# Cross-attention keys and queries projected with tokens on partitions, and attention root factors by token block

## The chip, the cores and the metric

The kernel runs on one core of one Trainium2 chip. TensorE (PE in the profile) multiplies, VectorE (DVE), ScalarE (ACT) and GpSimd (POOL) work on tiles of 128 partitions in SBUF, SyncE (SP) issues the loads. The metric is the device time of one execution in microseconds; of several runs the median counts.

## The reference, cut to what matters

One sequence of 256 tokens with 2048 features goes through two blocks: a feed-forward layer, a mixer of attention and gated linear attention, a cross-attention to 256 memory tokens, another feed-forward layer, a recurrent layer and a differential attention. The change touches the cross-attention and the norms of queries and keys in the two other attentions.

```python
def rms_norm(x, g):       # the second block's rms_norm_2 has the same form
    y = x * rsqrt(mean(x * x, axis=-1) + 1e-6)
    return y * g

def cross_attention(h, m, w_q, w_k, w_v, q_norm, k_norm, w_o):
    B, S, _ = h.shape
    M = m.shape[1]
    q = rms_norm((h @ w_q).reshape(B, S, N_XATTN_HEADS, HEAD_DIM).transpose(0, 2, 1, 3), q_norm)
    k = rms_norm((m @ w_k).reshape(B, M, N_XATTN_HEADS, HEAD_DIM).transpose(0, 2, 1, 3), k_norm)
    v = (m @ w_v).reshape(B, M, N_XATTN_HEADS, HEAD_DIM).transpose(0, 2, 1, 3)
    s = jnp.einsum("bhqd,bhkd->bhqk", q, k, preferred_element_type=jnp.float32) * (HEAD_DIM ** -0.5)
    p = jax.nn.softmax(s, axis=-1)
    o = jnp.einsum("bhqk,bhkd->bhqd", p, v.astype(jnp.float32)).astype(h.dtype)
    return o.transpose(0, 2, 1, 3).reshape(B, S, XATTN_W) @ w_o
# called with h = rms_norm(x, xattn_norm) and m = rms_norm(mem, mem_norm); 4 heads of 128
```

## The kernel before

All work hangs on weight units. A unit is 128 x 1024 of a weight matrix in fp32, 512 KB. SP loads it into one of four slots (`w_raw`, ring of four), ACT rounds it to its high half (`split`, L1034), DVE subtracts for the low half (L1510), and TensorE multiplies high by high, high by low and low by high. ACT and DVE are three units ahead of TensorE (`LEAD`); each engine's work that is not a split is put between the splits by the slot j of the unit at which its program names it. Semaphores (`handoffs`) pass results on, and every engine runs its own program strictly in order, so a wait on an engine holds all that stands behind it.

A projection has one of two forms. In the feature form (`unit`, `unit2`, L541 to L544) the weights are stationary and the result has features on partitions: for each of eight 128 x 128 tiles one matmul of 512 columns (high and low half of the activations) with the high weights, and one of 256 columns with the low ones. ACT then copies one half of the bank (`part_out`, L1054), DVE adds the other (`take`, L1533) and multiplies with the token's norm factor (L1535), which had to be spread over all partitions by a matmul of ones with a diagonal (`spread`, L631). In the token form (`unit_tokens`, L581 to L583) the activations are stationary and the result has tokens on partitions, one bank of 512 features for each of two token blocks b: twelve matmuls of 512 columns a unit.

In `cross`, memk (the keys' projection, 8 units) and xq (the queries', 8 units) have the feature form, and memv (the values', 8 units) the token form. Since keys and queries lie with features on partitions, the sum of squares over a head's features is a matmul with a column of ones (`sums`, L638, eight issues, sixteen records). For the keys POOL takes the root, DVE makes eight diagonals (L1978), TensorE spreads them (L949, two issues of 512 columns) and DVE multiplies the keys (L1926). For the queries the root stays by token and goes into the softmax: into the largest score (`largest`) and into the exponential's scale (`power`). The scores (L915) stand ahead of memv's unit 3, the turning of the probabilities (`turn`, L927) ahead of units 6 and 7, the mixes (L971) behind memv. Then comes xo, the output projection.

In both other attentions (mixa, four pairs of heads in 48 units, and att, eight iterations of 16 units) queries and keys already have tokens on partitions. The tables AT_A and AT_D set at which slot a step runs: "rope0" and "rope1" square (ACT) and rotate (DVE, L1687 to L1694) one token block each, "sum" reduces the squares of both blocks in one instruction (DVE, L1701) and adds the epsilon (L1703), POOL takes the root of all eight values (L2204), "scale" multiplies the keys by it (ACT, L1131, four instructions), "face" turns queries and keys (PE, eight transposes, L666).

## Time and profile before

| | us |
|---|---|
| median of 3 runs | 3347.47 |
| lowest, highest | 3344.51, 3347.66 |
| the profiled execution | 3342.44 |
| its span in the profile | 3340.7 |
| PE, DVE, ACT, POOL busy | 3288.2, 2234.1, 1719.0, 394.4 |
| mean granted clock of TensorE | 0.998 |

The span runs from the first to the last instruction, and the profiled execution took 1.7 us more than its span. A busy PE does not mean that it is at its peak: a matmul's end is modelled, and consecutive starts tell the step. Where the profile names a releaser, it is the one that came last.

### The profile page before, as it was taken

Reading aid. Unit: us, or ns where it says so; the run is one execution under the profiler, and the core shown is the slowest. Engines: PE = TensorE matmul, PEld = TensorE weight load, DVE = VectorE, ACT = ScalarE, POOL = GpSimd, SP = SyncE. Lnnn points to the kernel's source line nnn. Section 1 sums busy time; section 2 is a strip of 40 time slices with the busy share of each in tenths; the row PEclk is TensorE's granted clock in tenths of the full one; section 3 lists DMA queues with packets and bytes.
Section 4 is the critical chain, followed back from the end, with each engine's and each line's share of the span. In section 5 each row is a group of like instructions: output and inputs, shape, how many; then the busy total and the mean of one; then the engine's idle time right before and its main releaser. Section 6 shows DMA issues by size and latency. Waiting matters only on the chain.

```text
span 3340.7 us, 55144 instructions
## 1 busy us (share of the span) xinstructions
PE 3288.2 (98%) x18134; PEld 2829.4 (85%) x18134; DVE 2234.1 (67%) x3280; ACT 1719.0 (51%) x2554; POOL 394.4 (12%) x422
## 2 busy tenths in 40 slices
PE   8999999999999999999999999999999999999999
PEld 7888888887888878888888888888888888888888
DVE  7666666676655867666665677787556667665566
ACT  5444444455544655444444456774444445555554
POOL 1000000010023301000000001220333341100000
PEclk9999999999999999999999999999999999999999
DMA  6566666564555655566666655556545455555555
GB/s 229 185 201 184 192 189 189 184 188 145 170 158 163 195 152 161 186 189 187 189 190 188 187 178 178 192 176 189 160 155 156 152 157 177 178 168 176 170 169 164
DMA packets 273914, 592.48 MB, mean 177 GB/s; under 512 B 19856, under 2 KB 163472, under 8 KB 273696
## 3 DMA queue, kind: packets, MB, share of 16 engines
q1 hardware_dynamic: 272672, 587.12, 57.0%
q10 hardware_dynamic: 1152, 4.19, 0.3%
q8 instruction: 52, 0.85, 0.1%
q14 instruction: 38, 0.31, 0.0%
HBM read 589.14 MB, written 2.10 MB: 177 GB/s over the span
## 4 chain that ended last, share of the span: by engine, by line
PE 76%; issue 17%; DVE 4%; POOL 1%; ACT 1%; DMA 0%; SPq 0%; POOLq 0%; ACTq 0%
PE bank L542 42%; PE bank L541 10%; PE bank L544 10%; PE bank L581 3%; PE bank L583 3%; PE bank L582 3%; PE bank L769 2%; DVE w_low L1510 2%; PE bank L781 1%; DVE normed L1555 1%; POOL root_qk L2204 1%; ACT w_high L1034 1%; POOL work L2224 0%; DVE residual L1545 0%; PE bank L736 0%
## 5 line engine op out<-in xcount | busy, mean ns | idle before, releaser
L1510 DVE TENSOR_TENSOR w_low<-w_raw,w_high 128x1024 fp32r<-128x1024 f32 (+1 forms) x1120 | 1376.1, 1237 | 642.3 <-ACT w_high L1034 625.2
L1034 ACT ACTIVATE w_high<-w_raw 128x1024 fp32r<-128x1024 f32 (+1 forms) x1120 | 1166.5, 1044 | 777.2 <-PE bank L583 403.5
L542 PE MATMUL bank<-normed,w_high 128*128 128x512 f32 x4032 | 1286.4, 398 | 12.0 <-DVE w_low L1510 9.0
L542 PE MATMUL bank<-mixed,w_high 128*128 128x512 f32 x2496 | 791.6, 396 | 4.3 <-DVE increment L1542 4.3
L542 PEld LDWEIGHTS bank<-normed,w_high 128*128 128x128 f32 x4032 | 620.6, 189 | 13.6 <-issue 9.0
L541 PE MATMUL bank<-normed,w_low 128*128 128x256 f32 x2016 | 562.1, 279 | 0.0
L544 PE MATMUL bank<-normed,w_low 128*128 128x256 f32 x2016 | 560.0, 278 | 0.0
L541 PEld LDWEIGHTS bank<-normed,w_low 128*128 128x128 f32 x2016 | 379.3, 188 | 92.2
L581 PE MATMUL bank<-w_high,normed 128*128 128x512 f32 x1120 | 451.3, 403 | 2.0 <-DVE w_low L1510 1.1
L1054 ACT ACTIVATE parts<-bank 128x256 f32<-128x256 f32 x384 | 147.6, 384 | 592.0 <-PE bank L542 591.9
L544 PEld LDWEIGHTS bank<-normed,w_low 128*128 128x128 f32 x2016 | 380.0, 189 | 85.0
L583 PE MATMUL bank<-w_high,normed 128*128 128x512 f32 x1120 | 437.6, 391 | 0.0
L582 PE MATMUL bank<-w_low,normed 128*128 128x512 f32 x1120 | 437.0, 390 | 0.0
L542 PEld LDWEIGHTS bank<-mixed,w_high 128*128 128x128 f32 x2496 | 382.5, 189 | 6.8 <-issue 4.0
L541 PE MATMUL bank<-mixed,w_low 128*128 128x256 f32 x1248 | 347.4, 278 | 0.0
L544 PE MATMUL bank<-mixed,w_low 128*128 128x256 f32 x1248 | 346.1, 277 | 0.0
L541 PEld LDWEIGHTS bank<-mixed,w_low 128*128 128x128 f32 x1248 | 234.3, 188 | 57.0
L544 PEld LDWEIGHTS bank<-mixed,w_low 128*128 128x128 f32 x1248 | 234.7, 188 | 53.0 <-issue 0.2
L1533 DVE TENSOR_TENSOR increment<-bank,parts 128x256 f32<-128x256 f32 x252 | 106.9, 424 | 223.0 <-ACT parts L1054 223.0
L583 PEld LDWEIGHTS bank<-w_high,normed 128*128 128x128 f32 x1120 | 210.5, 188 | 45.3
L581 PEld LDWEIGHTS bank<-w_high,normed 128*128 128x128 f32 x1120 | 210.9, 188 | 42.9 <-issue 1.7
L582 PEld LDWEIGHTS bank<-w_low,normed 128*128 128x128 f32 x1120 | 211.1, 188 | 40.5
(293 smaller groups left out, 2291.5 us busy)
## 6 DMA issues: line engine op xcount, KB each, us to landing
w_raw<-w_att SPq DMA_DIRECT2D x128, 512.0 KB, 3.6
w_raw<-w_up1a SPq DMA_DIRECT2D x64, 512.0 KB, 4.2
w_raw<-w_up1b SPq DMA_DIRECT2D x64, 512.0 KB, 4.0
w_raw<-w_up2a SPq DMA_DIRECT2D x64, 512.0 KB, 4.0
w_raw<-w_up2b SPq DMA_DIRECT2D x64, 512.0 KB, 4.0
w_raw<-w_rg SPq DMA_DIRECT2D x64, 512.0 KB, 3.8
w_raw<-w_hg SPq DMA_DIRECT2D x64, 512.0 KB, 3.6
w_raw<-w_hg SPq DMA_DIRECT2D x128, 256.0 KB, 2.8
```

Source lines behind the costliest of these rows:

```text
L541: nc.tensor.matmul(banks[b][:, 0:S], lo, x[:, 0:S], start=False, stop=False)
L542: last = nc.tensor.matmul(banks[b][:, :], hi, x, start=starts and k == 0, stop=stop)
L544: last = nc.tensor.matmul(banks[b][:, 0:S], lo, x[:, 0:S], start=False, stop=False)
L581: nc.tensor.matmul(banks[b][:, :], x_hi, hi, start=starts and k == 0, stop=False)
L582: nc.tensor.matmul(banks[b][:, :], x_hi, lo, start=False, stop=False)
L583: last = nc.tensor.matmul(banks[b][:, :], x_lo, hi, start=False, stop=stops and k == UT // 4 - 1)
L769: last = nc.tensor.matmul(b_out[:, c * P:(c + 1) * P], B[:, 2 + hd, b * P:(b + 1) * P], rhs[:, hd, b * P:(b + 1) * P], start=True, stop=True)
L781: last = nc.tensor.matmul(b_out[:, n * S:(n + 1) * S], gw[:, t * P:(t + 1) * P], C[:, k, :], start=k == 0, stop=k == 1)
L1034: A_(wh[slot][:, 0:width], raw[slot][:, 0:width], ACT.Copy).then_inc(wh_done, 1)
L1054: A_(parts[b], banks[b][:, S:2 * S], ACT.Copy).then_inc(part_ready, 1)
L1510: TT(wl[slot][:, 0:width], raw[slot][:, 0:width], wh[slot][:, 0:width].bitcast(F32), ALU.subtract).then_inc(wl_done, 1)
L1533: TT(inc[:, b, :], gemm[b][:, 0:S], part[b], ALU.add).then_inc(evacuated, 1)
```

## The change

memk and xq go over to the token form. memk's banks are `mem_banks` = (p_a, p_b), xq's are `gemm`, and memv takes `mem_banks` again. `load_tokens` loads memk and xq in pieces as it did memv. Keys: ACT squares the two banks, DVE sums the squares by head and adds the epsilon (`row_sums`), which is scaled by the raw variance of the token (`row_eps`), so that the token's norm factor needs no multiplication at all; POOL takes the root of eight; DVE multiplies the banks by it into `key_rows`; TensorE turns them by eight transposes (`turn_rows`) ahead of xq's unit 5; ACT copies them to `KX`. Queries: ACT and DVE copy one bank each, ACT squares both, TensorE turns the unscaled rows ahead of memv's unit 1, ACT copies them with both gains as a scale, and the root stays by token. Both spreads, both column sums by matmul, the keys' diagonals and their spread, `part_out` and `take` of the two phases are gone. The steps from the scores on move forward by one unit of memv.

In both attentions "sum" becomes "sum0" and "sum1", one for each token block, with half the elements each: sum0 runs right behind rope0 and sum1 where sum was. POOL takes two roots of four values, and ACT's scaling waits for each block's own.

On PE in the cross-attention, the second place ahead of which a step of the keys stands (xq's units). Before, behind xq's unit 5 (L542 is the feature form; `diag` and `squares` hold the diagonals):

```order
L541 MATMUL bank<-mixed,w_low 128x256
L542 MATMUL bank<-mixed,w_high 128x512
L949 MATMUL bank<-diag,ones 128x512 [waits mem_diagonal]
L949 MATMUL bank<-squares,ones 128x512
L542 MATMUL bank<-mixed,w_high 128x512 [waits evacuated,wl_done]
L544 MATMUL bank<-mixed,w_low 128x256
```

After, behind xq's unit 4 (L584 to L586 are the token form, `constants` the identity, `work` the rows of keys):

```order
L584 MATMUL bank<-w_high,mixed 128x512
L585 MATMUL bank<-w_low,mixed 128x512
L586 MATMUL bank<-w_high,mixed 128x512
L939 MATMUL bank<-constants,work 128x128 [waits mem_scaled,rms_low]
L939 MATMUL bank<-constants,work 128x128 x7
L584 MATMUL bank<-w_high,mixed 128x512 [waits wl_done]
L585 MATMUL bank<-w_low,mixed 128x512
```

The matmuls of ones with the diagonals are gone, and eight transposes stand one unit earlier.

On PE at the beginning of memv. Before, the column sums stand behind its unit 1:

```order
L582 MATMUL bank<-w_low,normed 128x512
L583 MATMUL bank<-w_high,normed 128x512
L638 MATMUL bank<-ones,squares 128x1 [waits cross_squared,mem_varied]
L638 MATMUL bank<-ones,squares 128x1 x7
L581 MATMUL bank<-w_high,normed 128x512 [waits wl_done]
L582 MATMUL bank<-w_low,normed 128x512
```

After, the queries' transposes stand behind its unit 0, and the scores (L920) behind its unit 1:

```order
L586 MATMUL bank<-w_high,normed 128x512
L939 MATMUL bank<-constants,work 128x128 [waits cross_also_kept,cross_kept,rms_varied]
L939 MATMUL bank<-constants,work 128x128 x7
L584 MATMUL bank<-w_high,normed 128x512 [waits wl_done]
...
L586 MATMUL bank<-w_high,normed 128x512
L920 MATMUL bank<-mem_keys,work 128x256 [waits cross_gained,cross_squared,mem_keyed]
L920 MATMUL bank<-mem_keys,work 128x256 x3
L920 MATMUL bank<-mem_keys,work 128x256 [waits cross_gained]
L920 MATMUL bank<-mem_keys,work 128x256 x3
```

The column sums are gone; the transposes wait for the copies of the banks that xq's last unit has just finished.

On DVE in an iteration of att, slots 8 and 9. Before, from the last of rope0's products on:

```order
L1690 TENSOR_TENSOR diag<-bank,work 128x4x16
L75 REGISTER_ALU
L1694 TENSOR_TENSOR work<-work,diag 128x4x32 [waits dve_order]
...
L1687 TENSOR_TENSOR work<-bank,work 128x512 [waits att_squared]
L1688 TENSOR_TENSOR diag<-bank,work 128x4x16
L1690 TENSOR_TENSOR diag<-bank,work 128x4x16
...
L1694 TENSOR_TENSOR work<-work,diag 128x4x32 [waits dve_order]
...
L1510 TENSOR_TENSOR w_low<-w_raw,w_high 128x1024 [waits wh_done]
L1701 TENSOR_REDUCE sum_qk<-squares 128x8
...
L1703 TENSOR_TENSOR variance_qk<-sum_qk,eps_by_token 128x8 [waits dve_order]
...
L1510 TENSOR_TENSOR w_low<-w_raw,w_high 128x1024 [waits wh_done]
```

After:

```order
L1701 TENSOR_TENSOR diag<-bank,work 128x4x16
...
L1705 TENSOR_TENSOR work<-work,diag 128x4x32 [waits dve_order]
...
L1714 TENSOR_REDUCE sum_qk<-squares 128x4 [waits dve_order]
...
L1717 TENSOR_TENSOR variance_qk<-sum_qk,eps_by_token 128x4 [waits dve_order]
...
L1698 TENSOR_TENSOR work<-bank,work 128x512 [waits att_squared]
L1699 TENSOR_TENSOR diag<-bank,work 128x4x16
L1701 TENSOR_TENSOR diag<-bank,work 128x4x16
...
L1705 TENSOR_TENSOR work<-work,diag 128x4x32 [waits dve_order]
...
L1521 TENSOR_TENSOR w_low<-w_raw,w_high 128x1024 [waits wh_done]
L1714 TENSOR_REDUCE sum_qk<-squares 128x4
...
L1717 TENSOR_TENSOR variance_qk<-sum_qk,eps_by_token 128x4 [waits dve_order]
```

A reduction of four sums and an addition now stand between the two ropes, and behind the split of slot 9 only the second four are summed.

```diff
-        scores, mixes = (p_a, p_b, p_bc, p_o), (p_bc, p_o, p_t, p_sum)
+        scores, mixes = (*gemm, p_bc, p_o), (p_bc, p_o, p_t, p_sum)
+        mem_banks = (p_a, p_b)
...
-                                    *passes("wout"), ("memk", 8, 4), ("xq", 8, 4), ("memv", 8, 0), ("xo", 8, 0),
+                                    *passes("wout"), ("memk", 8, 0), ("xq", 8, 0), ("memv", 8, 0), ("xo", 8, 0),
...
-                16: [(("rope0", 1), 0)], 17: [(("rope1", 1), 0)], 18: [(("weigh", 0), 0)], 19: [(("sum", 1), 0)],
+                16: [(("rope0", 1), 0), (("sum0", 1), 0)], 17: [(("rope1", 1), 0)], 18: [(("weigh", 0), 0)], 19: [(("sum1", 1), 0)],
...
-                8: [("gate", 1), ("rope0", 0), ("rope1", 0)], 9: [("sum", 0)], 10: [("oturn", 1)], 11: [("scale", 0), ("store", 1)],
+                8: [("gate", 1), ("rope0", 0), ("sum0", 0), ("rope1", 0)], 9: [("sum1", 0)], 10: [("oturn", 1)], 11: [("scale", 0), ("store", 1)],
...
-                if name == "memv":
+                if name in ("memk", "xq", "memv"):
+                    row = 8 if name == "memv" else 0
                     for j in range(units):
-                        load_tokens(q0 + j // RING, j % RING, j // RING, 2 * (j % RING))
+                        load_tokens(q0 + j // RING, j % RING, src[row + j // RING:row + 8:2], 2 * (j % RING))
                     continue
...
+                def turn_rows(rows, banks, done):
+                    for hd in range(HEADS_X):
+                        for b in range(NB):
+                            last = nc.tensor.transpose(banks[hd // 2][:, hd % 2 * S + b * P:hd % 2 * S + (b + 1) * P],
+                                                       rows[:, b, hd * P:(hd + 1) * P], C_("ident"))
+                        if hd % 2:
+                            last.then_inc(done, 1)
...
                     normed("memk", j)
-                    if j == 2:
-                        spread(rms, NORMED["memk"], S)
                     if j == 4:
+                        pe.wait_ge(rms["varied"], NORMED["memk"] + 1)
                         sum_squares("xq")
-                    if j == 6:
-                        spread(rms, NORMED["xq"], S)
-                    unit2(q0, j, g0, XN, True)
+                    unit_tokens(q0 + j // RING, j % RING, 2 * j, XN, mem_banks, j == 0, j == 7)
...
-                    if j == 3:
-                        sums(mem, 0, [((t,), b) for t in range(4) for b in range(NB)])
-                    if j == 6:
-                        pe.wait_ge(mem["diagonal"], 1)
-                        for r in range(2):
-                            nc.tensor.matmul((p_bc, p_o)[r][:, :], ones[:, :], mem_diag[r], start=True,
-                                             stop=True).then_inc(mem["spread"], 1)
-                    unit2(q0, j, g0, Y, True)
+                    if j == 0:
+
+                        pe.wait_ge(evacuated, g0)
+                    if j == 5:
+                        pe.wait_ge(mem["scaled"], 2)
+                        turn_rows(key_rows, (p_bc, p_o), mem["turned"])
+                    unit_tokens(q0 + j // RING, j % RING, 2 * j, Y, gemm, j == 0, j == 7)
...
+                    if j == 1:
+                        pe.wait_ge(rms["varied"], NORMED["xq"] + 1)
+                        pe.wait_ge(crs["kept"], 1)
+                        pe.wait_ge(crs["also_kept"], 1)
+                        turn_rows(query_rows, (p_t, p_sum), crs["turned"])
                     if j == 2:
-                        pe.wait_ge(mem["varied"], 1)
-                        sums(crs, 0, [((t,), b) for t in range(4) for b in range(NB)])
-                    if j == 3:
                         for hd in range(HEADS_X):
                             score(hd)
-                    if j >= 6:
-                        turn(2 * j - 12)
-                        turn(2 * j - 11)
-                    unit_tokens(q0 + j // RING, j % RING, 2 * j, XN, gemm, j == 0, j == 7)
+                    if j in (5, 6):
+                        turn(2 * j - 10)
+                        turn(2 * j - 9)
+                    unit_tokens(q0 + j // RING, j % RING, 2 * j, XN, mem_banks, j == 0, j == 7)
...
-                    act.wait_ge(att["rooted"], it + 1)
                     for b in range(NB):
+                        act.wait_ge(att["rooted"], it * 2 + (b + 1))
...
-                    if j == 1:
-                        act.wait_ge(taken, g0 - takes["xq"])
-                        square(mem, 0, A[:, :, :], 4)
-                    if evacuates("xq", j, True):
-                        k = j - 2 if j < RING else j // 2
-                        part_out(q0, j, g0 + k, k % 2)
+                    if j == 0:
+                        act.wait_ge(pe_unit, q0 * RING)
+                        for b in range(NB):
+                            A_(sq[:, 2 * b:2 * b + 2, :], mem_banks[b][:, :], ACT.Square).then_inc(mem["squared"], 1)
+                    if j == 5:
+                        for r in range(2):
+                            act.wait_ge(mem["turned"], r + 1)
+                            A_(KX[:, 2 * r:2 * r + 2, :], (p_bc, p_o)[r][:, :], ACT.Copy).then_inc(mem["keyed"], 1)
                 q0, g0, _, _ = place["memv"]
                 for j in range(8):
                     ahead("memv", q0, j, 8, True)
                     if j == 0:
-                        act.wait_ge(taken, g0 - takes["memv"])
-                        act.wait_ge(mem["summed"], 1)
-                        square(crs, 0, B[:, :, :], 4)
-                        A_(Dm[:, :, :], B[:, :, :], ACT.Copy, scale=V_("xattn_q_norm")).then_inc(crs["gained"], 1)
-                    if j in (4, 5):
-                        power(2 * j - 8)
-                        power(2 * j - 7)
-                    if j >= 6:
-                        copy_probs(2 * j - 12)
-                        copy_probs(2 * j - 11)
+                        act.wait_ge(pe_unit, q0 * RING)
+                        A_(query_rows[:, 0, :], gemm[0][:, :], ACT.Copy).then_inc(crs["kept"], 1)
+                        for b in range(NB):
+                            if b:
+                                act.wait_ge(crs["also_kept"], 1)
+                            A_(sq[:, 2 * b:2 * b + 2, :], gemm[b][:, :], ACT.Square).then_inc(crs["squared"], 1)
+                    if j == 1:
+                        for r in range(2):
+                            act.wait_ge(crs["turned"], r + 1)
+                            A_(Dm[:, 2 * r:2 * r + 2, :], (p_t, p_sum)[r][:, :], ACT.Copy,
+                               scale=cross_gain[:, 0:1]).then_inc(crs["gained"], 1)
+                    if j in (3, 4):
+                        power(2 * j - 6)
+                        power(2 * j - 5)
...
-                if step == "sum":
-                    own.did(nc.vector.reduce_sum(sum_qk[:, :], sq[:, :, :].rearrange("p a (c d) -> p (a c) d", c=2), AX.X))
-                    own.settle()
-                    TT(var_qk[:, :], sum_qk[:, :], eps_qk[:, :], ALU.add).then_inc(att["varied"], 1)
+                if step in ("sum0", "sum1"):
+                    b = int(step[-1])
+                    of = slice(4 * b, 4 * b + 4)
+                    own.did(nc.vector.reduce_sum(sum_qk[:, of], sq[:, 2 * b:2 * b + 2, :].rearrange("p a (c d) -> p (a c) d", c=2),
+                                                 AX.X))
+                    own.settle()
+                    TT(var_qk[:, of], sum_qk[:, of], eps_qk[:, of], ALU.add).then_inc(att["varied"], 1)
...
+                def row_eps(name, dst):
+
+                    dve.wait_ge(rms["rooted"], NORMED[name])
+                    variance(rms, NORMED[name], [(0, NB)], [1.0 / D], [EPS])
+                    dve.wait_ge(rms["varied"], NORMED[name] + 1)
+                    own.did(TS(dst[:, :].rearrange("p (b c) -> p b c", b=NB), var[:, 0:NB].unsqueeze(2).broadcast_to([P, NB, 4]),
+                               P * EPS, None, ALU.mult))
+                    own.settle()
+
+                def row_sums(h, eps):
+
+                    dve.wait_ge(h["squared"], 2)
+                    own.did(nc.vector.reduce_sum(sum_qk[:, :], sq[:, :, :].rearrange("p a (c d) -> p (a c) d", c=2), AX.X))
+                    own.settle()
+                    TT(var_qk[:, :], sum_qk[:, :], eps[:, :], ALU.add).then_inc(h["varied"], 1)
...
+                    if j == 1:
+                        row_sums(mem, eps_qk)
                     if j == 3:
-                        variance(mem, 0, [(0, 8)], [1.0 / P], [EPS])
-                    if j == 5:
                         dve.wait_ge(mem["rooted"], 1)
-                        for c in range(8):
-                            last = TS(mem_diag[c // 4][:, c % 4 * P:(c % 4 + 1) * P], C_("ident"), rstd[:, c:c + 1],
-                                      None, ALU.mult)
-                        last.then_inc(mem["diagonal"], 1)
-                    if j >= 6:
-                        keys(j - 6)
+                        for b in range(NB):
+                            TT(key_rows[:, b, :].rearrange("p (h d) -> p h d", h=HEADS_X),
+                               mem_banks[b].rearrange("p (h d) -> p h d", h=HEADS_X),
+                               root_qk[:, 4 * b:4 * b + 4].unsqueeze(2).broadcast_to([P, HEADS_X, P]),
+                               ALU.mult).then_inc(mem["scaled"], 1)
...
+                    if j == 0:
+                        dve.wait_ge(pe_unit, q0 * RING)
+                        nc.vector.tensor_copy(query_rows[:, 1, :], gemm[1][:, :]).then_inc(crs["also_kept"], 1)
+                    if j == 1:
+                        row_sums(crs, eps_x)
+                    if j in (2, 3):
+                        largest(2 * j - 4)
+                        largest(2 * j - 3)
+                    if j in (4, 5):
+                        weigh(2 * j - 8)
+                        weigh(2 * j - 7)
...
-                pool.wait_ge(att["varied"], it + 1)
-                PT_(root_qk[:, :], var_qk[:, :], mhalf[:, :], ALU.pow).then_inc(att["rooted"], 1)
+                for b in range(NB):
+                    of = slice(4 * b, 4 * b + 4)
+                    pool.wait_ge(att["varied"], it * 2 + (b + 1))
+                    PT_(root_qk[:, of], var_qk[:, of], mhalf[:, of], ALU.pow).then_inc(att["rooted"], 1)
```

## Rows read from the trace of the kernel before

**Rows 1.** Page, part 1; windows view (length, busy by engine, granted clock, DMA).
```profile
PE 3288.2 (98%) x18134; PEld 2829.4 (85%) x18134; DVE 2234.1 (67%) x3280; ACT 1719.0 (51%) x2554; POOL 394.4 (12%) x422
...
1216.00:1220.00 4.00, 3.95 (x9) 2.08 (x10) 1.87 (x2) 0.00 (x0) 0.00 (x0) 0.63 0.37 113
```

**Rows 2.** PE timeline, cross-attention: start us, us, operation, count, [idle before, releaser].
```profile
1174.91 0.39 PE L542 MATMUL bank<-normed,w_high 128*128 128x512 f32 x1
1176.29 0.67 PE L631 MATMUL bank<-diag,ones 128*128 128x256 f32 x2 [0.98 <-DVE diag L1629]
1176.61 0.58 PE L542 MATMUL bank<-normed,w_high 128*128 128x512 f32 x1
...
1202.78 1.84 PE L638 MATMUL bank<-ones,squares 128*128 128x1 f32 x16
...
1212.70 0.39 PE L542 MATMUL bank<-mixed,w_high 128*128 128x512 f32 x1
1216.05 2.08 PE L949 MATMUL bank<-diag,ones 128*128 128x512 f32 x2 [2.96 <-DVE squares L1978]
1217.92 1.54 PE L949 MATMUL bank<-squares,ones 128*128 128x512 f32 x2
...
1224.63 0.40 PE L542 MATMUL bank<-mixed,w_high 128*128 128x512 f32 x1
1225.97 0.50 PE L581 MATMUL bank<-w_high,normed 128*128 128x512 f32 x1 [0.93 <-DVE increment L1533]
```

**Rows 3.** Timeline of DVE, POOL, ACT and PE, one iteration of att.
```profile
2931.22 1.22 DVE L1701 TENSOR_REDUCE sum_qk<-squares 128x8 f32<-128x1024 f32 x1
2932.47 0.17 DVE L1703 TENSOR_TENSOR variance_qk<-sum_qk,eps_by_token 128x8 f32<-128x8 f32 x1
2932.57 1.23 DVE L1510 TENSOR_TENSOR w_low<-w_raw,w_high 128x1024 fp32r<-128x1024 f32 x1
...
2932.72 2.57 POOL L2204 TENSOR_TENSOR root_qk<-variance_qk,minus_half 128x8 f32<-128x8 f32 x1 [10.57 <-DVE variance_qk L1703]
...
2933.04 1.06 ACT L1034 ACTIVATE w_high<-w_raw 128x1024 fp32r<-128x1024 f32 x1 [2.12 <-PE bank L583]
2935.32 1.28 ACT L1131 ACTIVATE work<-work,root_qk 128x128 f32<-128x128 f32 x4 [1.22 <-POOL root_qk L2204]
...
2935.34 0.39 PE L583 MATMUL bank<-w_high,normed 128*128 128x512 f32 x1
2936.65 1.09 PE L666 MATMUL bank<-constants,work 128*128 128x128 f32 x8 [0.93 <-ACT work L1131]
```

**Rows 4.** PE waits of 2760 to 3260 us: us in total, times, longest.
```profile
PE bank L666 <- ACT work L1131: 7.0, 8, 0.9
```

**Rows 5.** PE timeline: the feature form in memk, then the token form in memv.
```profile
1169.57 0.40 PE L542 MATMUL bank<-normed,w_high 128*128 128x512 f32 x1
...
1243.01 0.39 PE L581 MATMUL bank<-w_high,normed 128*128 128x512 f32 x1
1247.55 0.39 PE L583 MATMUL bank<-w_high,normed 128*128 128x512 f32 x1
```

**Rows 6.** Loads of 1150 to 1262 us: count, KB, median us to landing.
```profile
w_raw<-w_mem SPq DMA_DIRECT2D x16, 512.0 KB, 3.6
```

**Rows 7.** Groups by line (busy us, mean ns, idle before); DVE timeline.
```profile
L927 PE MATMUL bank<-constants,work 128*128 128x128 f32 x16 | 2.3, 279 | 2.4 <-DVE work L1948 2.3
...
2939.61 0.69 DVE L1706 COPY work<-bank 128x512 f32<-128x512 f32 x1
```

**Rows 8.** POOL timeline: a root of eight, and a root of four.
```profile
792.02 1.64 POOL L2204 TENSOR_TENSOR root_qk<-variance_qk,minus_half 128x8 f32<-128x8 f32 x1 [31.67 <-DVE variance_qk L1703]
...
2398.63 1.01 POOL L2230 TENSOR_TENSOR root_heads<-variance_heads,minus_half 128x4 f32<-128x4 f32 x1 [13.73 <-DVE variance_heads L1796]
```

**Rows 9.** PE timeline of mixa, second half of its units.
```profile
882.11 1.09 PE L666 MATMUL bank<-constants,work 128*128 128x128 f32 x8 [1.40 <-ACT work L1131]
...
903.83 0.87 PE L682 MATMUL bank<-constants,work 128*128 128x128 f32 x6 [0.22 <-DVE work L1733]
```

99 lines of the change are left out of this document (39 added, 60 removed).

## The prediction, made before the changed kernel ran

> **What bounds the kernel now.** I read the page first: TensorE is busy for 98% of the span [rows 1], so time is saved only where TensorE stands still or does work that can go. Next the waits of PE, which say where it stands still, then PE's timeline round the cross-attention, where two consecutive starts give the true step (a matmul's modelled end overlaps the next start by 0.16 us), and last the other engines' timelines round each wait. In the cross-attention the reader is to see four interruptions between units that are none of the projection's work [rows 2]. In both other attentions it is one and the same wait: PE stands before the transposes of L666 for ACT's scaling, and ACT stands for POOL's root [rows 3, 4].
>
> **Keys and queries in token form: the units themselves.** Sixteen units change form. A feature unit is 8 x (512 + 256) columns, a token unit 12 x 512: the same 6144. Two feature units take 5.34 + 0.23 = 5.57 us, 2.785 each; in the token form 20 steps take 4.54 us, 0.227 each, 2.72 a unit [rows 5]. Just behind foreign work the token step is nearer 0.23, so I take 0.05 instead of 0.065: 16 x 0.05 = 0.8 us gained, bounds 0 and 1.0. The loads of memk and xq get memv's form; the sixteen loads of `w_mem`, eight of each form, have a median of 3.6 us to landing against the lead of a ring of four units [rows 6]: nothing.
>
> **What goes from PE's path.** (a) The first spread: 0.98 us of wait, 0.16 of overlap, 0.32 of matmul, 1.5 in all; the second has no wait, 0.3 [rows 2]. What is late next is unit 3's low half, whose split stands ahead of this wait in DVE's program; the splits behind it come earlier too, since DVE loses its own wait for POOL's root. (b) The column sums L638, twice 1.84 us of busy time, 1.7 each on the path: 3.4. (c) The keys' spread: from 1212.93 (last matmul 1212.70 + 0.23) to 1219.3 (1217.92 + 1.54 less the overlap), 6.4 us, 3.1 of it waiting for DVE's eight diagonals, the rest four matmuls at a granted clock of 0.63 [rows 1, 2]. (d) The wait for the last evacuation ahead of memv, 1225.97 - 1224.86 = 1.1 [rows 2]. Sum (a) to (d) with the units: 1.8 + 3.4 + 6.4 + 1.1 + 0.8 = 13.5 us.
>
> **What comes onto it.** Sixteen transposes. Eight L666 transposes are busy for 1.09 us [rows 3], sixteen L927 for 2.3 [rows 7]: 1.0 per eight with the start, 2.0 in all, bounds 1.7 and 16 x 0.279 = 4.5, were none to overlap the next. I take the low side, for the same instruction overlaps in both rows. The Trainium skill (TensorE: Matmul & The Clock Gate, Part 4: PE-mode transpose) gives about 275 ns for one 128x128 transpose in a kernel; by that the sixteen would cost 4.4 us and the whole would gain 2.4 us less. The rows show 279 ns as the duration of one too, but 2.3 us for sixteen.
>
> The keys' chain hides behind five units. From the end T of memk: ACT waits for its split of the next unit (1.06) and squares two banks, T+2.4; DVE reaches the row sums behind its second split, T+5.3, and is done at T+6.8; POOL's root of eight takes at most 2.6 [rows 3], T+9.4; DVE's third split ends T+10.7, and two products of 0.7 each (a bank copy is 0.69 [rows 7]) end T+12.0. PE asks at T + 5 x 2.73 = T+13.7. Slack 1.7 us: cost nothing; if the cover were gone, every further microsecond would be PE's. The queries have less cover: PE asks after one memv unit, U+2.73. There DVE first does its split (behind ACT's, U+0.26+1.06+1.2 = U+2.5) and then the bank copy, U+3.2: a wait of 0.5 us, bounds 0.2 and 1.0, and behind it on PE stand all later units. The scores then start at U+6.9, the scaled queries are there at U+5.9. The score's and weighing's steps move forward by one unit together, so the 2.3 us wait before L927 [rows 7] stays. Net for the cross-attention: 13.5 - 2.0 - 0.5 = 11.0 us.
>
> **Sums and roots by block, last attention.** Eight iterations, 7.0 us of idle in all [rows 4], plus 8 x 0.16 overlap: 8.3 us. The chain now, in one iteration [rows 3]: sum 2931.22, small add 2932.47, DVE's next split at 2932.57, POOL's root 2932.72 to 2935.29, four scalings 2935.32 to 2936.60, PE 2936.65, while PE was free at 2935.57. The root of eight took 2.57 us here but 1.64 where no split had started before it, and a root of four 1.01 [rows 8]; so a root of four costs 1.01, at most 1.01 + 0.93. After: sum 0 with its add sits ahead of rope 1 and pushes DVE by 0.64 + 0.14 = 0.8; sum 1 is 0.6 shorter, so the split starts 0.2 later, at 2932.8. POOL is held until about 2933.85 and done at 2934.9. ACT has its split done at 2934.07 [rows 3], scales block 0 until 2934.7 and block 1 from 2934.9 to 2935.55. PE is asked at 2935.6 instead of 2936.65: 0.05 us of wait is left. Gain 8.3 - 0.4 = 7.9, bounds 6 and 8.3. DVE's 0.8 us is hidden by the lead of three units that its splits have.
>
> **The same in the first attention.** Four pairs, one of which waits: 1.40 + 0.16 = 1.6 us gone [rows 9]. But for odd pairs sum 0 comes at slot 16, ahead of the weighing at slot 18, for which PE waits 0.22 us at 903.83 already [rows 9]: it waits 0.8 to 0.9 more there once; the other odd pair has just 0.9 of slack. Net 0.7, bounds -0.5 and 1.6.
>
> **Sum.** 11.0 + 7.9 + 0.7 = 19.6 us. The profiled execution took 3342.44 us, 5.0 under the median of the three runs shown (3347.47); against itself it would be 3322.8, and taken off the median 3327.9. I give 3328. What the measurement can tell from no change is about 0.2%, 6.7 us.
>
> **Rivals.** (1) Only the cross-attention gains: POOL's second root still ends late, because DVE's extra work and the held port eat what the shorter sum gives. For it: POOL and DVE hold each other up already (2.57 against 1.64). Against: the deadline is met by the sum above even at the dear price of a root. 3347.5 - 11 = 3336.5. Chance 0.10.
> (2) The keys miss their slack and PE stands for 3 us again, and as at 1216 to 1220 the clock falls from the level of 2.4 GHz to that of 1.2 GHz in part of the stretch [rows 1]: 3 us plus 1 for the eight transposes and the next matmuls, 3332. For it: five engine handovers in a row. Against: 1.7 us of slack. 0.10.
> (3) Transposes that don't overlap: 16 x (0.279 - 0.125) = 2.5 us, 3330.5; against it stand [rows 3, 7]. 0.05.
> (4) The cross-attention's gain is given back in xo, where DVE has a split, two additions and two low halves in every unit, and only the attentions gain: 3347.5 - 8.6 = 3339. Against: DVE's lead over PE is capped by the ring, so DVE does not fall behind when PE comes earlier. 0.05.
> (5) Slower: DVE becomes the bound of the attentions' iterations. Each gets 0.8 us of DVE work more, and POOL's new root of 1.01 us can hold a split or an add up in full: 1.8 x 12 = 21.7 us, and the root comes no earlier, so only the 11 stand against it: 3347.5 + 10.7 = 3358. It decides from the point where a split ends more than its three units (8.2 us) late. Against it: DVE is busy for 67% of the span [rows 1], and 1.8 us in an iteration of 16 units (44 us) is 4% more. 0.03. The Trainium skill (SBUF - State Buffer, Who interferes with whom) has the rule that a DVE instruction with two SBUF inputs and a GpSimd one that reads SBUF shut each other out, whichever starts first; the two prices of a root agree with it on POOL's side, and the rows show no DVE instruction held.
>
> **How the numbers follow.** The forecast has 0.67: 3328. The bounds of its terms (2.5 up for the transposes, 2 for the attention's remainder, 1.2 in the first attention; down 1 to 3) give 3324 to 3333. The range is to hold eight in ten and a run's own scatter of 3 us: 3320 to 3339, which takes in rivals 1 to 3. Faster by over 0.2% is all but rival 5, some of rival 4 and what I don't see: 0.93; within 0.2%: 0.04; slower: 0.03.
>
> **What would show it.** Right: from memk's first matmul to the mixes ahead of xo it takes some 11 us less; no matmul with ones between memk's first unit and xo but the one sum of squares; the clock at 1.00 all through; POOL's roots of four at 1.0 to 1.9 us, PE idle before the transposes of the last attention under 0.1 us each. Wrong would be: a PE wait before the keys' transposes, one over 1 us before the queries', or DVE's splits in the attentions starting later than PE asks for them.

## The result, and the profile after

The changed kernel takes 3325.60 us (median of 4 runs, 3324.63 to 3327.11) against 3346.08 us before (4 runs, 3344.51 to 3347.66): ratio 0.9941, 95% interval 0.9928 to 0.9953, 20.5 us less. Predicted were 3328, 19.6 less. The profiled execution took 3327.11 us, its span is 3325.3.

The first line of the page on engines (busy us, share of the span, instructions) answers to [rows 1]: 88 matmuls fewer, PE now at 99%.

```profile
PE 3284.4 (99%) x18046; PEld 2828.9 (85%) x18046; DVE 2231.8 (67%) x3282; ACT 1716.5 (52%) x2550; POOL 401.4 (12%) x434
```

The time in stages, each from the first matmul of one line to the first of the next (L602 at its second place, at some 1165 us), the last stage to the last matmul of L666, from the PE rows of all profiles. The lines are those of the kernel before; the changed ones have L721, L605, L979, L1023 and L669 for them.

| us | first attention, gated linear (L718 to L602) | cross-attention (L602 to L971) | middle (L971 to L1015) | last attention (L1015 to the last L666) |
|---|---|---|---|---|
| before | 383.6 | 93.5 | 1593.3 | 379.9 |
| changed | 383.3 | 83.2 | 1595.3 | 372.1 |
| difference | -0.3 | -10.3 | +2.0 | -7.8 |
| predicted | -0.7 | -11.0 | 0 | -7.9 |

Ahead of L718 the changed kernel's profile is 1.0 us later (its first matmul starts 1.6 later). That is scatter: L718 starts between 781.8 and 783.6 us in the thirteen profiles of this case, whatever the kernel. So the two profiled executions differ by 15.3 us, the medians by 20.5: the profiled execution of before lies 3.6 us below its median, that of the changed kernel 1.5 above. The stages explain the 15.3.

The granted clock says which executions of before were profiled. Of the 29 whose clock is on record, the 12 at 0.998 took 3341.7 to 3343.8 us, the 16 at 0.997 took 3344.5 to 3346.4 and the one at 0.996 took 3347.8. Both profiles of before (3342.44 and, in experiment 9, 3343.33 us) are of the first group. The slower executions have more time at the lower clock; where in the kernel, no profile shows.

**Cross-attention.** PE's waits from 1160 to 1290 us (engine, line, releaser: us in total, times, longest), changed kernel:

```profile
PE bank L932 <- DVE work L1966: 2.3, 1, 2.3
PE bank L545 <- DVE increment L1553: 1.4, 2, 1.1
PE bank L979 <- DVE mem_values L2011: 0.9, 1, 0.9
...
PE bank L939 <- DVE work L2000: 0.4, 1, 0.4
```

Of the four interruptions of [rows 2] none is left: no diagonal, no column sum between units, no wait for the last evacuation ahead of memv. The one new wait is that of the queries' transposes (L939), 0.4 us; the keys' transposes wait for nothing. Their places in the changed kernel's timelines of DVE and PE (start us, us, operation, [idle before, releaser]):

```profile
1203.17 1.28 DVE L1991 TENSOR_TENSOR work<-bank,root_qk 128x512 f32<-128x512 f32 x2
...
1205.89 0.39 PE L586 MATMUL bank<-w_high,mixed 128*128 128x512 f32 x1
1206.12 1.04 PE L939 MATMUL bank<-constants,work 128*128 128x128 f32 x8
1206.91 0.48 PE L584 MATMUL bank<-w_high,mixed 128*128 128x512 f32 x1
...
1218.49 1.07 PE L939 MATMUL bank<-constants,work 128*128 128x128 f32 x8 [0.44 <-DVE work L2000]
```

DVE has the scaled keys at 1204.45 and PE asks at 1206.12: 1.7 us of slack. From the transposes' start to the next matmul it takes 0.79 us.

**What the prediction did not have: the clock.** Windows of the changed kernel (window, length, busy by engine, granted clock, DMA share, GB/s):

```profile
1190.00:1213.00 23.00, 23.00 (x107) 19.14 (x106) 14.24 (x18) 11.52 (x15) 1.64 (x1) 1.00 0.60 185
1213.00:1235.00 22.00, 20.53 (x95) 16.66 (x93) 11.80 (x17) 12.89 (x23) 1.64 (x1) 1.00 0.48 144
1235.00:1240.00 5.00, 3.65 (x15) 2.84 (x16) 4.40 (x14) 3.35 (x9) 0.00 (x0) 0.77 0.37 117
1240.00:1245.00 5.00, 5.00 (x25) 4.19 (x24) 1.31 (x2) 2.03 (x3) 0.00 (x0) 0.89 0.24 93
```

The fall at 1216 to 1220 us of [rows 1] is gone with the wait ahead of it. But behind the 2.3 us wait ahead of the turning of the probabilities (L927 before, L932 now), where the profile of before has 1.00, the clock now falls. PE's timeline there:

```profile
1236.28 1.38 PE L932 MATMUL bank<-constants,work 128*128 128x128 f32 x8 [2.31 <-DVE work L1966]
1237.42 0.57 PE L584 MATMUL bank<-w_high,normed 128*128 128x512 f32 x1
1237.79 0.63 PE L585 MATMUL bank<-w_low,normed 128*128 128x512 f32 x1
...
1241.15 0.40 PE L584 MATMUL bank<-w_high,normed 128*128 128x512 f32 x1
```

From 1237.42 to 1241.15 nine steps take 3.73 us instead of 9 x 0.227 = 2.04: the fall to the level of 1.2 GHz, where a step takes 0.43 us, costs 1.7 us. A second one stands in the middle stage, at 2251 us, behind a wait of 1.8 us for DVE's addition (L1553). Windows of the changed kernel, then its PE timeline:

```profile
2249.00:2251.00 2.00, 0.19 (x1) 0.22 (x2) 1.93 (x5) 1.33 (x2) 0.00 (x0) 1.00 0.66 240
2251.00:2253.00 2.00, 2.00 (x8) 1.68 (x8) 1.97 (x5) 0.00 (x0) 0.00 (x0) 0.60 0.00 0
2253.00:2255.00 2.00, 2.00 (x8) 1.70 (x7) 1.19 (x2) 0.00 (x0) 0.00 (x0) 0.54 0.76 199
```

```profile
2250.81 0.47 PE L545 MATMUL bank<-mixed,w_high 128*128 128x512 f32 x1 [1.81 <-DVE increment L1553]
...
2251.36 1.00 PE L545 MATMUL bank<-mixed,w_high 128*128 128x512 f32 x2
```

Before, the same wait stands at the same place of the program (2260.14 us there), and behind it the clock stays, as its timeline and a window show:

```profile
2260.14 0.47 PE L542 MATMUL bank<-mixed,w_high 128*128 128x512 f32 x1 [1.83 <-DVE increment L1542]
```

```profile
2260.00:2265.00 5.00, 4.86 (x28) 4.32 (x29) 4.73 (x8) 1.34 (x2) 0.00 (x0) 1.00 0.48 128
```

There is a third difference, in the same stage. At a wait of 3.9 us that ends at 2038 us (2028 in the changed kernel) the clock falls in both kernels, before for 3.4 us. In this execution of the changed kernel it stays down for 6.8, in the repeated one of experiment 4 for 3.4 again. Windows of the one, then of the other:

```profile
2026.10:2029.55 3.45, 1.55 (x4) 1.28 (x5) 2.22 (x6) 0.30 (x2) 0.71 (x1) 0.51 0.72 247
2029.55:2033.00 3.45, 3.45 (x13) 2.97 (x12) 2.06 (x3) 1.31 (x3) 0.00 (x0) 0.51 0.71 211
```

```profile
2028.40:2031.90 3.50, 3.50 (x13) 3.01 (x12) 2.06 (x3) 1.07 (x2) 0.00 (x0) 0.51 0.78 265
2031.90:2036.00 4.10, 4.10 (x25) 3.58 (x25) 3.23 (x7) 2.26 (x3) 0.00 (x0) 1.00 0.62 144
```

**Last attention.** PE's wait of [rows 4], 7.0 us before, is gone from the list of 2740 to 3260 us. One iteration of the changed kernel, timelines of DVE, POOL, ACT and PE as in [rows 3]:

```profile
2923.68 0.68 DVE L1714 TENSOR_REDUCE sum_qk<-squares 128x4 f32<-128x512 f32 x1
2924.39 0.16 DVE L1717 TENSOR_TENSOR variance_qk<-sum_qk,eps_by_token 128x4 f32<-128x4 f32 x1
2924.49 2.59 DVE L1521 TENSOR_TENSOR w_low<-w_raw,w_high 128x1024 fp32r<-128x1024 f32 x2
...
2921.49 1.01 POOL L2222 TENSOR_TENSOR root_qk<-variance_qk,minus_half 128x4 f32<-128x4 f32 x1 [7.62 <-DVE variance_qk L1717]
2924.63 1.95 POOL L2222 TENSOR_TENSOR root_qk<-variance_qk,minus_half 128x4 f32<-128x4 f32 x1 [2.14 <-DVE variance_qk L1717]
...
2925.73 0.68 ACT L1139 ACTIVATE work<-work,root_qk 128x128 f32<-128x128 f32 x2
2926.61 0.69 ACT L1139 ACTIVATE work<-work,root_qk 128x128 f32<-128x128 f32 x2 [0.20 <-POOL root_qk L2222]
...
2927.06 0.39 PE L586 MATMUL bank<-w_high,normed 128*128 128x512 f32 x1
2927.36 1.09 PE L669 MATMUL bank<-constants,work 128*128 128x128 f32 x8
```

The first root is free of the second sum, the second starts as DVE's split starts and takes the dear price, and it is done in time: ACT's last scaling ends at 2926.61 + 0.69 = 2927.30, PE is through with its unit at 2927.06 + 0.23 = 2927.29 and starts at 2927.36.

### The profile page after: what moved, and what is told of

The parts are those of the page before. It is cut to its first block, busy times and chain, and to the rows that moved or that the text cites. A ratio compares the mean times of both kernels' runs of the same rounds, so it can differ in the third digit from the quotient of the medians.

```text
span 3325.3 us, 54997 instructions
## 1 busy us (share of the span) xinstructions
PE 3284.4 (99%) x18046; PEld 2828.9 (85%) x18046; DVE 2231.8 (67%) x3282; ACT 1716.5 (52%) x2550; POOL 401.4 (12%) x434
## 4 chain that ended last, share of the span: by engine, by line
PE 90%; issue 4%; DVE 3%; ACT 1%; POOL 1%; DMA 0%; SPq 0%; ACTq 0%; POOLq 0%; DVEq 0%
PE bank L545 41%; PE bank L544 10%; PE bank L547 10%; PE bank L584 8%; PE bank L586 8%; PE bank L585 8%; PE bank L772 2%; DVE w_low L1521 1%; PE bank L784 1%; DVE normed L1566 1%; ACT w_high L1042 1%; POOL work L2242 0%; PE bank L739 0%; PE bank L669 0%; DMA w_raw<-w_up1a 0%
## 5 line engine op out<-in xcount | busy, mean ns | idle before, releaser
L545 PE MATMUL bank<-normed,w_high 128*128 128x512 f32 x3968 | 1266.5, 398 | 13.0 <-DVE w_low L1521 10.6
L545 PE MATMUL bank<-mixed,w_high 128*128 128x512 f32 x2432 | 772.2, 397 | 4.2 <-DVE increment L1553 4.2
L544 PE MATMUL bank<-normed,w_low 128*128 128x256 f32 x1984 | 554.1, 279 | 0.0
L547 PE MATMUL bank<-normed,w_low 128*128 128x256 f32 x1984 | 551.8, 278 | 0.0
L584 PE MATMUL bank<-w_high,normed 128*128 128x512 f32 x1152 | 464.9, 404 | 1.1 <-DVE w_low L1521 1.1
L586 PE MATMUL bank<-w_high,normed 128*128 128x512 f32 x1152 | 451.5, 392 | 0.0
L585 PE MATMUL bank<-w_low,normed 128*128 128x512 f32 x1152 | 450.8, 391 | 0.0
L544 PEld LDWEIGHTS bank<-normed,w_low 128*128 128x128 f32 x1984 | 373.4, 188 | 90.2
L547 PEld LDWEIGHTS bank<-normed,w_low 128*128 128x128 f32 x1984 | 375.6, 189 | 83.0
L545 PEld LDWEIGHTS bank<-mixed,w_high 128*128 128x128 f32 x2432 | 373.3, 189 | 6.2 <-issue 3.8
L544 PE MATMUL bank<-mixed,w_low 128*128 128x256 f32 x1216 | 339.2, 279 | 0.0
L547 PE MATMUL bank<-mixed,w_low 128*128 128x256 f32 x1216 | 337.9, 278 | 0.0
L544 PEld LDWEIGHTS bank<-mixed,w_low 128*128 128x128 f32 x1216 | 228.6, 188 | 55.1
L547 PEld LDWEIGHTS bank<-mixed,w_low 128*128 128x128 f32 x1216 | 229.9, 189 | 51.3
L586 PEld LDWEIGHTS bank<-w_high,normed 128*128 128x128 f32 x1152 | 217.1, 188 | 46.6
L584 PEld LDWEIGHTS bank<-w_high,normed 128*128 128x128 f32 x1152 | 217.7, 189 | 43.0 <-issue 1.7
```

Source lines behind the costliest of these rows:

```text
L544: nc.tensor.matmul(banks[b][:, 0:S], lo, x[:, 0:S], start=False, stop=False)
L545: last = nc.tensor.matmul(banks[b][:, :], hi, x, start=starts and k == 0, stop=stop)
L547: last = nc.tensor.matmul(banks[b][:, 0:S], lo, x[:, 0:S], start=False, stop=False)
L584: nc.tensor.matmul(banks[b][:, :], x_hi, hi, start=starts and k == 0, stop=False)
L585: nc.tensor.matmul(banks[b][:, :], x_hi, lo, start=False, stop=False)
L586: last = nc.tensor.matmul(banks[b][:, :], x_lo, hi, start=False, stop=stops and k == UT // 4 - 1)
```

## The experiments

Each is an edit of the changed kernel or that kernel itself, except the second and the ninth, which start from the kernel before.

**1. Only the cross-attention.** The tables, sums, roots and scalings of both attentions are as before; two places of the edit:

```diff
-                8: [("gate", 1), ("rope0", 0), ("sum0", 0), ("rope1", 0)], 9: [("sum1", 0)],
+                8: [("gate", 1), ("rope0", 0), ("rope1", 0)], 9: [("sum", 0)],
...
+                    act.wait_ge(att["rooted"], it + 1)
```

> The changed kernel with both attentions as before (one sum of eight, one root of eight). Theory 1, each part saves what its own waits were: the stretch from memk's first matmul to the mixes of L971's kind is about 10 us shorter than in the kernel before, as after the change, and PE again idles about 7.0 us in eight waits before the last attention's transposes: 11 to 12 us faster than before in all. Theory 2, the cross-attention's gain is given back in xo and behind: under 6 us faster. The wait of 2.3 us before the turning of the probabilities stays; if the clock falls behind it again, as in the changed kernel, the cross-attention's own layout does it; if it stays at 1.00, it is chance, and the stretch is 1.7 us shorter still.

Measured: 3333.50 us (3331.49 to 3337.20) against 3344.97 for before, ratio 0.9968 (0.9957 to 0.9980), 11.5 less: theory 1. Stages 383.8, 83.2, 1593.5, 380.3; PE stands 7.4 us in eight waits before the last attention's transposes. The clock falls behind the 2.3 us wait here too (at 1236.9 us).

**2. Only the attentions.** The kernel before with that other half of the change; one place of it, its line cut at the end:

```diff
-                8: [("gate", 1), ("rope0", 0), ("rope1", 0)], 9: [("sum", 0)],
+                8: [("gate", 1), ("rope0", 0), ("sum0", 0), ("rope1", 0)], 9: [("sum1", 0)],
```

> The kernel before with the sums and roots by token block in both attentions and nothing else. Theory 1: the last attention saves 7.9 us (its waits before the transposes under 0.1 us each), the first one 0.3 to 0.7, so 8 to 9 us faster than before. Theory 2, the extra reduction and POOL's second root slow DVE and give part back elsewhere: under 5 us faster. PE's wait for the weighing in the first attention grows from 0.2 to 1.0 us by either.

Measured: 3336.18 us (3334.91 to 3337.41), ratio 0.9975 (0.9965 to 0.9985), 8.8 less. Stages 383.2, 95.0, 1592.9, 372.1. The halves add up to 11.5 + 8.8 = 20.3 us, against 20.5 for the whole in the first comparison and 18.6 in this one (experiment 4); the difference of 1.7 lies within the intervals. The cross-attention, whose program is untouched here, takes 95.0 instead of 93.5, for here the clock falls behind the same 2.3 us wait. So experiment 1's layout alone does not make it fall, which its expectation had as the test. Windows of this kernel:

```profile
1245.00:1250.00 5.00, 4.47 (x20) 3.38 (x18) 2.97 (x6) 4.97 (x12) 0.00 (x0) 1.00 0.36 108
1250.00:1255.00 5.00, 3.22 (x12) 2.86 (x13) 4.41 (x13) 4.06 (x11) 0.00 (x0) 0.69 0.33 105
```

So with the fall on both sides the new cross-attention is 95.0 - 83.2 = 11.8 us shorter (12.0 against the 83.0 of experiment 10); against before, with the full clock behind that wait, it is 10.3.

**3. Two sums, one root.** DVE sums by block as changed, POOL takes one root of eight behind the second, ACT waits for it.

```diff
-                for b in range(NB):
-                    of = slice(4 * b, 4 * b + 4)
-                    pool.wait_ge(att["varied"], it * 2 + (b + 1))
-                    PT_(root_qk[:, of], var_qk[:, of], mhalf[:, of], ALU.pow).then_inc(att["rooted"], 1)
+                pool.wait_ge(att["varied"], it * 2 + 2)
+                PT_(root_qk[:, :], var_qk[:, :], mhalf[:, :], ALU.pow).then_inc(att["rooted"], 1)
```

> The changed kernel, but POOL waits for both sums and takes one root of eight, and ACT's scaling waits for that one. It asks which part of the change in the attentions saves the wait. Theory 1, the two roots do it: a root of eight behind the split costs 2.6 us instead of 1.9, and all four scalings (1.28 us) come behind it instead of two, so PE's wait before the transposes comes back at 1.0 to 1.3 us in each of eight iterations: 8 to 10 us slower than the changed kernel. Theory 2, the shorter last sum does it (0.5 us): then 4 us slower at most.

Measured: 3334.59 us (3332.17 to 3336.56), ratio 0.9970 (0.9957 to 0.9982), 8.2 more than the changed kernel in the same comparison. Stages of the profile: 83.0, 1593.4 and 381.5 for the last attention, 1.6 more than before and 1.2 more than in experiment 1, which has the same cross-attention and one sum. Its waits from 2740 to 3260 us, and one iteration on POOL, ACT and PE:

```profile
PE bank L669 <- ACT work L1139: 8.6, 8, 1.1
```

```profile
2923.55 2.58 POOL L2220 TENSOR_TENSOR root_qk<-variance_qk,minus_half 128x8 f32<-128x8 f32 x1 [10.75 <-DVE variance_qk L1717]
...
2926.16 1.28 ACT L1139 ACTIVATE work<-work,root_qk 128x128 f32<-128x128 f32 x4 [1.41 <-POOL root_qk L2220]
...
2927.49 0.77 PE L669 MATMUL bank<-constants,work 128*128 128x128 f32 x5 [1.12 <-ACT work L1139]
```

The root's end and the four scalings behind it are the whole wait. Splitting the sum alone makes it longer. The gain is that half of the scaling no longer waits for the second root (0.69 us behind it instead of 1.28) and that this root has four columns (1.95 instead of 2.58).

**4. The changed kernel again**, in the same comparison.

> The changed kernel once more, beside the others on the same chip. 20 us faster than before. It asks whether the clock's fall behind the 2.3 us wait before the turning of the probabilities, and the one at the start of the second recurrent half, come again. Theory 1, chance: the clock is at 1.00 in one of the two places, and the span is 1 to 3 us shorter. Theory 2, it belongs to the new layout: the same fall at the same place.

Measured: 3326.34 us (3325.66 to 3327.39), ratio 0.9946 (0.9929 to 0.9963). It gains 18.6 us here, not the 20 expected. Stages 383.0, 83.2, 1594.7, 372.1: both falls of the clock are there again, but the one at 2028 us lasts 3.4 us, not 6.8, and the middle stage is 0.6 shorter.

**5. The probabilities turned one unit later**, so that PE does not stand for the softmax.

```diff
-                    if j in (5, 6):
-                        turn(2 * j - 10)
-                        turn(2 * j - 9)
+                    if j in (6, 7):
+                        turn(2 * j - 12)
+                        turn(2 * j - 11)
```

(and `copy_probs` on ACT likewise)

> The changed kernel with the turning of the probabilities (PE) and their copies (ACT) one unit of memv later, ahead of units 6 and 7 as in the kernel before; the weighing stays where the change put it. Theory 1: the wait of 2.3 us before the turning goes, and with it the fall of the clock that came behind it in the changed kernel and in three of the four runs made since (e2 too, which has the old layout), so the stretch from memk to the mixes is 3.5 to 4.5 us shorter than in the changed kernel and the whole 3 to 5 us faster. Theory 2, the copies then come late for the mixes: a new wait ahead of L979, and no gain.

Measured: 3322.14 us (3321.12 to 3323.96) against 3345.34, ratio 0.9933 (0.9918 to 0.9948). Cross-attention 78.9, 4.3 less than 83.2. In its windows and PE timeline the wait is gone and the clock stays:

```profile
1235.00:1240.00 5.00, 5.00 (x28) 4.07 (x27) 4.40 (x15) 3.86 (x8) 0.00 (x0) 1.00 0.52 127
```

```profile
1236.09 1.13 PE L932 MATMUL bank<-constants,work 128*128 128x128 f32 x8
```

The wait's 2.3 and the fall's 1.7 are 4.0 of the 4.3 us. The fall in the middle stage is there all the same (1595.3). The expectation has the fall in three of the four runs made before; their traces show it in all four.

**6. The first attention's odd pairs: sum0 behind the weighing.**

```diff
-                16: [(("rope0", 1), 0), (("sum0", 1), 0)], 17: [(("rope1", 1), 0)], 18: [(("weigh", 0), 0)],
+                16: [(("rope0", 1), 0)], 17: [(("rope1", 1), 0)], 18: [(("weigh", 0), 0), (("sum0", 1), 0)],
```

> The changed kernel with the first attention's sum 0 of odd pairs at slot 18 behind the weighing, not at slot 16 ahead of it. Theory 1: PE's wait of 1.0 us before the turning of the weights (L685) falls to 0.2 and the whole is 0.8 us faster, within what can be told. Theory 2, sum 1 one slot later now makes the root late: a wait before the transposes of L669 takes its place, same time.

Measured: 3324.16 us (3322.84 to 3325.28), ratio 0.9937 (0.9922 to 0.9952); by the medians 1.4 to 2.2 less than the changed kernel, within the intervals. The stage decides: 381.6 us against 383.3 and 383.0. The changed kernel's PE timeline, then this one's list of waits from 740 to 930 us:

```profile
881.97 1.04 PE L669 MATMUL bank<-constants,work 128*128 128x128 f32 x8
...
904.44 0.77 PE L685 MATMUL bank<-constants,work 128*128 128x128 f32 x5 [1.01 <-DVE work L1747]
```

```profile
PE bank L685 <- DVE work L1747: 0.2, 1, 0.2
```

**7. Both moves (5 and 6).**

> The two moves of e5 and e6 together. Theory 1: 4 to 5.5 us faster than the changed kernel, 24 to 26 faster than before. Theory 2 (either move brings a new wait): under 3 us faster than the changed kernel.

Measured, in five rounds: 3320.96 us (3319.04 to 3321.33), ratio 0.9927 (0.9914 to 0.9941), 24.4 less than before. Stages 381.6, 78.9, 1595.7, 372.2. It is the best version that ran.

**8. The keys turned twice.** Eight more transposes of the same rows, into banks that are written anew later, ahead of the real ones.

```diff
+                        for hd in range(HEADS_X):
+                            for b in range(NB):
+                                nc.tensor.transpose((p_bc, p_o)[hd // 2][:, hd % 2 * S + b * P:hd % 2 * S + (b + 1) * P],
+                                                    key_rows[:, b, hd * P:(hd + 1) * P], C_("ident"))
```

> The changed kernel with eight more transposes of the keys ahead of the eight that count. It prices eight transposes on TensorE's path by themselves. Theory 1, consecutive transposes overlap: from the first to the next unit's first matmul 0.8 us more than in the changed kernel. Theory 2, the rule of about 275 ns each (the Trainium skill, TensorE: Matmul & The Clock Gate, Part 4: PE-mode transpose) holds for each in a row: 2.2 us more.

Measured: 3325.84 us, one time. The eight additional ones are L961 in its PE timeline:

```profile
1205.10 1.03 PE L961 MATMUL bank<-constants,work 128*128 128x128 f32 x8
1205.97 1.04 PE L939 MATMUL bank<-constants,work 128*128 128x128 f32 x8
1206.77 0.48 PE L584 MATMUL bank<-w_high,mixed 128*128 128x512 f32 x1
```

Eight transposes occupy PE for 0.80 to 0.87 us, 0.1 each. The Trainium skill (TensorE: Matmul & The Clock Gate, Part 4: PE-mode transpose) gives about 275 ns for one; in this trace that is the duration of one from start to end (0.272 us in the middle), and of eight in a row each costs 0.10 to 0.11. By an estimate from the page's figure, 8 x 0.275, the eight would have added 2.2 us; they added 0.87.

**9 to 11. Who owns the falls?** Three kernels once more, unchanged: before, only the cross-attention, and two sums with one root.

> The kernel before, unchanged. Its first profile shows the granted clock at 1.00 behind the 2.3 us wait ahead of the probabilities' turning (L927), where the profiles of six kernels built from it show the clock fall to 0.63 to 0.77 for some 3 us. If the fall belongs to that wait and the first profile was the exception, this one shows it: cross-attention 95.1 us from first to last, as with only the attentions changed, instead of 93.4. If it belongs to the changed kernels, the cross-attention takes 93.4 again and the clock stays at 1.00. Behind the 1.8 us wait in the middle stage the clock stays at 1.00 by both.

> Only the cross-attention changed, unchanged from its first run. There the clock stayed at 1.00 behind the 1.8 us wait of the middle stage, and the stage took 1593.5 us; with both changes it took 1594.7 to 1595.7 and the clock fell in five profiles of five. If the fall comes by the execution, it can show here too (stage 1595); if it belongs to the two roots, it does not (1593.5).

> The changed kernel with one root of eight instead of two of four, unchanged from its first run: middle stage 1593.4 us there, the clock at 1.00 behind the 1.8 us wait. If the fall comes by the execution, it can show here (1595); if it belongs to the two roots, it does not. Last attention 381.5 again by both.

Measured, one time each: 3343.33, 3333.12 and 3334.69 us, with 3342.02 for before beside them. Stages: before again 384.0, 93.7, 1593.4, 379.9; only cross 383.6, 83.0, 1593.5, 380.3; one root 383.8, 83.0, 1593.5, 381.4. My guess that the first profile of before was an exception fell, as far as a second profile from the same group of executions, those at 0.998, can say. In the repeated one, PE's timeline and a window:

```profile
1251.07 1.38 PE L927 MATMUL bank<-constants,work 128*128 128x128 f32 x8 [2.31 <-DVE work L1948]
```

```profile
1250.00:1255.00 5.00, 3.86 (x20) 3.12 (x21) 4.28 (x14) 3.14 (x9) 0.00 (x0) 1.00 0.46 125
```

The same 2.31 us wait, the same full clock behind it, as in the first. And the middle stage of the repeated kernel with one root, timeline and window:

```profile
2250.60 0.47 PE L545 MATMUL bank<-mixed,w_high 128*128 128x512 f32 x1 [1.82 <-DVE increment L1553]
```

```profile
2250.00:2255.00 5.00, 4.40 (x25) 3.89 (x26) 4.76 (x9) 1.47 (x3) 0.00 (x0) 1.00 0.38 129
```

At these two waits each kernel that was profiled twice repeated its pattern. At the middle stage's wait the clock fell in all six profiles of kernels with both changes (the changed kernel twice, experiments 5 to 8) and in none of seven others (before twice, attentions alone, cross alone twice, one root twice). The wait's length does not tell them apart (1.81 to 1.84 us in all), nor does the time at which it ends, counted from the start of the span: 2249.66 and 2250.81 have the fall, 2250.14 and 2250.60, between them, do not.

Counted from another point, the time does put them in order. Take the moment at which the clock last rose, at the end of the fall that begins between 2020 and 2041 us, and count from there to the start of the wait. In the six profiles with the fall it is 215.45 to 216.51 us, in the seven without it 216.55 to 216.94; the two nearest the edge are experiments 8 and 1. The wait of 2.3 us in the old layout goes the same way: the clock fell in experiment 2, where the wait begins 28.3 us behind the last rise, and stayed in both profiles of before, at 28.8 and 29.0. In the new layout the last rise lies some 420 us back, and the clock fell in all eight profiles with the wait. This orders every case on record, but the edge is narrow and no edit moved a wait across it: it is an ordering, not a cause shown. It would explain why a kernel repeats its pattern, since the program sets the time from one fall to the next wait, and why an edit elsewhere changes it.

**An estimate with the clock taken out.** At the lower level a step takes about twice as long (0.43 us, not 0.227). So take off each stage half of the time in which PE works at that level, read from each profile. For the first attention that time is the work behind a wait of 5.9 us at 803 to 809 us, behind which the clock is low in every profile. It differs between executions, here in the changed kernel and in experiment 7:

```profile
809.01:814.40 5.39, 5.39 (x15) 4.45 (x16) 3.64 (x9) 0.80 (x1) 0.00 (x0) 0.50 0.30 97
```

```profile
808.61:812.55 3.94, 3.94 (x11) 3.33 (x12) 2.23 (x5) 0.80 (x1) 0.00 (x0) 0.50 0.14 50
```

| us, estimate | first attention | cross-attention | middle |
|---|---|---|---|
| before (2 profiles) | 381.2 | 92.0 | 1591.6 to 1591.7 |
| only cross (2) | 381.2, 381.3 | 81.5, 81.3 | 1591.8 |
| changed (2) | 380.6, 380.5 | 81.5 | 1591.1, 1591.3 |
| sum behind the weighing (experiments 6, 7) | 379.7 | 81.5, 78.9 | 1590.9 |

The profiles of one kernel, which differ by up to 0.6 us as measured, now agree within 0.3, in the first attention within 0.1.

## Why the prediction was right, and where it was not

**Interruptions removed, 13.5 us, less 2.5 added: net 11.0.** With the fall behind the 2.3 us wait on both sides the cross-attention gained 11.8 to 12.0 (experiment 2 against 1 and 10). Each term was a little pessimistic: eight transposes cost 0.8 instead of 1.0, 0.4 in all; the queries' wait was 0.44 instead of 0.5; 16 units at the full 0.065 us of [rows 5] give 0.24 more. The rest of 0.1 to 0.3 was not traced. The keys' slack was forecast as 1.7 and is 1.7; the loads hid as said.

**"The clock at 1.00 all through": wrong.** This is the step that failed. I took the 2.3 us wait as a thing that stays and costs the same before and after. It stayed, but a fall of the clock came behind it that the profiles of before do not have, worth 1.7 us: 12.0 - 1.7 = 10.3, the stage's 10.3. The middle stage, on which I had not looked at all, is 2.0 longer (1595.3 against 1593.3). The fall behind its 1.8 us wait costs 1.7 by the estimate, and the fall at 2026 us, twice as long in this execution, 0.8; the work without them is 0.5 shorter, which was not traced. So the clock took 4.2 us in the two stages, against no fall forecast, and the middle gave 0.5 back. The second rival had the right mechanism (a wait, then the lower level) with a price of 3 + 1 us, but at the wrong place: it had the keys miss their slack.

**Last attention, 7.9 us: right, by its own chain.** Stage 379.9 to 372.1, 7.8 less. The second root was held as forecast: 1.95 us, of 1.01 + 0.93 at most, and 0.07 us of idle time is left where 0.05 was forecast. POOL's roots of four over the kernel (count, min/median/max ns):

```profile
L2222 POOL TENSOR_TENSOR root_qk<-variance_qk,minus_half x24: 1006/1922/1951, 783.6 to 3213.1; 128x4 f32<-128x4 f32 x24
```

The Trainium skill (SBUF - State Buffer, Who interferes with whom) has it that a DVE instruction with two SBUF inputs and a GpSimd one that reads SBUF shut each other out; POOL's two prices, 1.01 alone and 1.95 started just behind a split, agree. DVE's side does not: the second of the two splits in the row at 2924.49 starts at 2925.86, while the root runs until 2926.58, and takes its usual 1.23 us. Experiment 3 excludes the other reading, that the gain comes from the shorter sum.

**First attention, 0.7 us net: right, once the clock is taken out.** The wait of 1.40 [rows 9] is gone, as the row at 881.97 above shows; at 903.83 the wait of 0.22 grew to 1.01, by 0.8 as forecast. As measured the stage gained only 0.3 (0.6 in experiment 4), with 0.4 between the two profiles of before. By the estimate it gained 0.6 to 0.7, from 381.2 to 380.5 and 380.6. In the same way, moving the sum behind the weighing brought 1.4 to 1.7 as measured and 0.8 to 0.9 by the estimate, about the 0.8 that its wait shows.

**The sum.** 19.6 us forecast; the medians give 20.5, the two profiled executions 15.3. The terms are those of a profile, so the latter is the honest comparison for them: 4.3 us are missing, 2.0 in the middle stage (the clock), 1.0 ahead of the first stage (scatter), 0.7 in the cross-attention (12.0 gained, 1.7 lost, 11.0 forecast), 0.4 in the first attention (the clock again) and 0.1 in the last. That the medians agree better is partly luck: 5 us of scatter of the executions against their medians stand between. Most executions of before are slower and at a lower clock than the two that were profiled, and the forecast had no term for that. The forecast of 3328 also started from a median of 3347.5; with a fourth run it is 3346.1, and the gain is 0.9 larger than forecast.

**Rivals.** Only the cross-attention gains (3336.5): excluded, experiment 2 gains 8.8 without it. Transposes that do not overlap (3330.5): excluded by experiment 8. Given back in xo (3339): excluded, the stage from the mixes on takes 1593.5 us with only the cross-attention changed, 1593.3 before. DVE as the bound (3358): excluded, there is no wait for a split in the last attention.
